# The prompt's down products of an expert in one run of sixteen matmuls, with two buffers of raw down weights

## What is computed

```python
def ec_moe(h, w_router, w_g, w_u, w_d):
    B, n, D = h.shape
    cap = EC_FACTOR * n // N_EXPERTS          # 256 sample tokens, 32 prompt tokens
    aff = jax.nn.softmax((h @ w_router).astype(jnp.float32), axis=-1)
    vals, idx = lax.top_k(aff.transpose(0, 2, 1), cap)
    xg = jax.vmap(lambda hb, ib: hb[ib])(h, idx)
    a = jnp.einsum('becd,edf->becf', xg, w_g)
    u = jnp.einsum('becd,edf->becf', xg, w_u)
    y = jnp.einsum('becf,efd->becd', jax.nn.silu(a) * u, w_d) * vals[..., None].astype(h.dtype)
    ...
```

## Time and profile before

| | us |
|---|---|
| median of 3 runs | 3077.3 (3075.81 to 3077.61) |
| span of the profiled execution | 3073.1 |
| PE busy in it | 2897.7 (94%) |
| PE's weight loads busy | 2284.8 (74%) |
| DVE busy | 1953.7 (64%) |
| ACT busy | 1085.5 (35%) |
| POOL busy | 1070.6 (35%) |

### The profile page before, as it was taken

The page is one execution under the profiler, slowest core; times in us unless marked ns, Lnnn a source line. Parts: engine busy times, 40 slices in busy tenths (PEclk is TensorE's granted clock), DMA queues, the critical chain, the costliest instruction groups (busy, mean ns, idle before and its releaser), DMA issues. The chain is left out here.

```text
span 3073.1 us, 42659 instructions
## 1 busy us (share of the span) xinstructions
PE 2897.7 (94%) x16288; PEld 2284.8 (74%) x16288; DVE 1953.7 (64%) x2559; ACT 1085.5 (35%) x1723; POOL 1070.6 (35%) x693
## 2 busy tenths in 40 slices
PE   6999999999889999999999999989977999999993
PEld 3888888888676666666666667878856888888882
DVE  5418292829438888888888866555575555555555
ACT  5311111111344444444444443223432333434344
POOL 1000000000105343443433554522136766666652
PEclk9999999999898999999999999999988999999996
DMA  6213222211441110110110117675534666666657
GB/s 235 102 50 108 79 102 79 100 73 61 171 152 32 27 33 7 32 33 7 34 26 6 55 53 226 182 248 179 168 135 140 199 205 200 194 204 211 205 186 291
DMA packets 139518, 371.25 MB, mean 121 GB/s; under 512 B 20886, under 2 KB 47996, under 8 KB 129116
## 3 DMA queue, kind: packets, MB, share of 16 engines
q1 hardware_dynamic: 99756, 266.55, 26.0%
q0 software_dynamic: 24048, 74.72, 8.6%
q10 hardware_dynamic: 15552, 27.79, 2.6%
HBM read 266.07 MB, written 102.89 MB: 120 GB/s over the span
## 5 line engine op out<-in xcount | busy, mean ns | idle before, releaser
L1209 ACT ACTIVATE at_w<-banks 128x512 f32<-128x512 f32 (+1 forms) x592 | 347.6, 591 | 463.6 <-PE banks L1316 407.9
L1432 DVE TENSOR_REDUCE at_mpart<-banks 128x1 f32<-128x512 f32 (+1 forms) x584 | 373.7, 682 | 136.5 <-PE banks L1343 136.5
L1288 POOL TENSOR_TENSOR at_part<-at_part,at_w 128x512 f32<-128x512 f32 x224 | 297.6, 1329 | 327.2 <-ACT at_w L1209 323.9
L2705 POOL TENSOR_TENSOR late<-moe_raw_gu,late 128x2048 fp32r<-128x2048 f32 x62 | 287.2, 4633 | 121.6 <-ACT late L2770 121.3
L536 DVE SCALAR_TENSOR_TENSOR fr_r<-fr_r,fr_dw 128x2334 f32<-128x2334 f32 x120 | 318.0, 2650 | 3.9
L393 PE MATMUL fr_po<-hT_hi,fr_w_hi 128*128 128x512 f32 (+1 forms) x800 | 297.3, 372 | 3.0 <-PE fr_po L393 1.8
L393 PE MATMUL fr_po<-hT_hi,fr_w_lo 128*128 128x512 f32 (+1 forms) x800 | 294.9, 369 | 0.0
L393 PE MATMUL fr_po<-hT_lo,fr_w_hi 128*128 128x512 f32 (+1 forms) x800 | 294.9, 369 | 0.0
L1354 PE MATMUL banks<-at_w,V 128*64 128x256 f32 (+1 forms) x2368 | 283.0, 381 | 0.0
L2897 DVE TENSOR_TENSOR late<-raw,late 128x1024 fp32r<-128x1024 f32 x64 | 192.0, 3001 | 100.8 <-ACT late L2809 100.8
L1458 DVE TENSOR_TENSOR at_part<-at_part,at_w 128x512 f32<-128x512 f32 x224 | 231.5, 1033 | 13.0
(11 more groups left out here) (404 smaller groups left out, 6295.6 us busy)
## 6 DMA issues: line engine op xcount, KB each, us to landing
moe_raw_gu<-w_gate_up SPq DMA_DIRECT2D x62, 1024.0 KB, 4.8
raw<-w_down SPq DMA_DIRECT2D x64, 512.0 KB, 4.0
fr_wm<-w_ada_rows POOLq DMA_DIRECT2D x32, 512.0 KB, 4.3
gates_scratch<-fr_r ACTq DMA_DIRECT2D x64, 256.0 KB, 2.0
mx_gates<-gates_scratch SPq DMA_DIRECT2D x64, 256.0 KB, 3.1
fr_raw<-w_in SPq DMA_DIRECT2D x28, 512.0 KB, 5.5
fr_r<-x POOLq DMA_DIRECT2D x18, 512.0 KB, 5.5
raw<-mixed_scratch SPq DMA_DIRECT2D x9, 1024.0 KB, 6.0
```

What stands on the lines that cost most here:

```text
L1209: act.activation(w[:, g % NW, k, 0:n], sc[:, (2 * g + k) % SCB, 0:n], ACT.Exp, scale=SM_SCALE).then_inc(exp_done, 1)
L1288: pool.tensor_tensor(part[:, j % 2, 1, 0:n], before, w[:, g % NW, 1, 0:n], ALU.add).then_inc(add_p, 1)
L1432: dve.tensor_reduce(mpart[:, s, tiles, c // 2], bank, AX.X, ALU.max).then_inc(red_done, 1)
L2705: pool.tensor_tensor(gu_lo[:, slot], raw_gu[:, slot], gu_hi[:, slot].bitcast(F32), ALU.subtract).then_inc(glo_done, 1)
```

## The change

The prompt's down products leave steps 1, 2 and 3. In step 0 of the next expert, behind the last piece's `down`, `down_prompt` now makes those of all four pieces in one run of 16 matmuls, still accumulating in `moe_y`, and raises the new semaphore `prompt_mm`. `d_mm` is raised by the last matmul of `down`. Since weights and activations must last until then, there is a second buffer of raw down weights (`raw_d[u]`) and `hid` holds four pieces of two experts. Room for it comes from the final phase: four of its nine tiles lie in `raw_d[0]`, and ACT's squares go to parts of `xg` and `hid`. SP's transfer of down weights waits for `prompt_mm` of two experts earlier in place of `d_mm`; `scale_y` waits for `prompt_mm`; the first `hid` of an expert waits for `prompt_mm` too.

```diff
-        gu_hi, gu_lo, raw_d = expert_buffers(raw, late)
+        gu_hi, gu_lo, raw_d0 = expert_buffers(raw, late)
+        raw_d = [raw_d0, p.sb("raw_d1", [P, M, D])]
...
-        act_g, hid = p.sb("act_g", [P, TOK]), p.sb("hid", [P, 2, TOK])
+        act_g, hid = p.sb("act_g", [P, TOK]), p.sb("hid", [P, 2, M, TOK])
...
-        fx, fsq = p.sb("fx", [P, U, D]), p.sb("fsq", [P, 2, D])
+        fx = p.sb("fx", [P, U - M, D])
+        fsq = [xg[:, 2], hid[:, 0].rearrange("p m n -> p (m n)")[:, 0:D]]
...
-                        sp.wait_ge(d_mm, q - 3)
-                        sp.dma_start(raw_d[:, m], t["w_down"][bass.ds(q * P, P), :]).then_inc(d_ld[m], 16)
+                        if not isinstance(e, int) or e > 1:
+                            sp.wait_ge(prompt_mm, e - 1)
+                        sp.dma_start(raw_d[u][:, m], t["w_down"][bass.ds(q * P, P), :]).then_inc(d_ld[m], 16)
...
                 def scale_y(e, u):
-                    dve.wait_ge(d_mm, M * e + M)
+                    dve.wait_ge(prompt_mm, e + 1)
...
+                        if m == 0 and (not isinstance(e, int) or e > 1):
+                            dve.wait_ge(prompt_mm, e - 1)
+                        dve.tensor_tensor(hid[:, u, m], bank[1][:, 0:TOK], act_g[:], ALU.mult).then_inc(hid_done, 1)
...
-                def down_prompt(slot, piece):
-
-                    for g in range(4):
-                        mm = pe.matmul(y3[g * CAPP:(g + 1) * CAPP, :], hid[:, slot, CAP:TOK], raw_d[:, piece, g * QD:(g + 1) * QD],
-                                       start=(piece == 0), stop=(piece == M - 1), skip_group_check=True)
                     mm.then_inc(d_mm, 1)
+
+                def down_prompt(u):
+
+                    for piece in range(M):
+                        for g in range(4):
+                            mm = pe.matmul(y3[g * CAPP:(g + 1) * CAPP, :], hid[:, u, piece, CAP:TOK],
+                                           raw_d[u][:, piece, g * QD:(g + 1) * QD],
+                                           start=(piece == 0), stop=(piece == M - 1), skip_group_check=True)
+                    mm.then_inc(prompt_mm, 1)
...
-                        if not (first and m == 0):
-                            down_prompt(1 - slot, (m - 1) % M)
+                        if m == 0 and not first:
+                            down_prompt(1 - u)
```

More of the change, by code:

```diff
@@ L2590, in moe_phase @@
         tp_done, xhi_done, xlo_done = p.sem("tp_done"), p.sem("xhi_done"), p.sem("xlo_done")
-        g_mm, u_mm, d_mm = p.sem("g_mm"), p.sem("u_mm"), p.sem("d_mm")
+        g_mm, u_mm, d_mm, prompt_mm = p.sem("g_mm"), p.sem("u_mm"), p.sem("d_mm"), p.sem("prompt_mm")
         silu_done, hid_done, hhi_done, hlo_done, y_done = (
@@ L2620, in buffer @@
             at = place_of(n)
-            return fx[:, at] if at < U else raw_gu[:, (at - U) // 2, (at - U) % 2].rearrange("p k n -> p (k n)")
+            if at < M:
+                return raw_d0[:, at]
+            return fx[:, at - M] if at < U else raw_gu[:, (at - U) // 2, (at - U) % 2].rearrange("p k n -> p (k n)")
         def wait_tab(eng, e):
@@ L2781, in squares @@
                     wait(act, sq_done, n - 1)
-                    act.activation(fsq[:, n % 2], buffer(n), ACT.Square, accum_out=sumsq[:, n:n + 1]).then_inc(sq_done, 1)
+                    act.activation(fsq[n % 2], buffer(n), ACT.Square, accum_out=sumsq[:, n:n + 1]).then_inc(sq_done, 1)
                 def rooted(n):
@@ L2808, in expert @@
                             act.wait_ge(d_mm, q - 1)
-                        act.activation(d_hi[:, slot], raw_d[:, m], ACT.Copy).then_inc(dhi_done, 1)
+                        act.activation(d_hi[:, slot], raw_d[u][:, m], ACT.Copy).then_inc(dhi_done, 1)
                         if last and m == M - 1:
@@ L2815, in expert @@
                         act.wait_ge(hid_done, q + 1)
-                        act.activation(h_hi[:, slot], hid[:, slot, 0:CAP], ACT.Copy).then_inc(hhi_done, 1)
+                        act.activation(h_hi[:, slot], hid[:, u, m, 0:CAP], ACT.Copy).then_inc(hhi_done, 1)
                         if m > 0 and not last:
@@ L2896, in expert @@
                         dve.wait_ge(dhi_done, q + 1)
-                        dve.tensor_tensor(d_lo[:, slot], raw_d[:, m], d_hi[:, slot].bitcast(F32), ALU.subtract
+                        dve.tensor_tensor(d_lo[:, slot], raw_d[u][:, m], d_hi[:, slot].bitcast(F32), ALU.subtract
                                           ).then_inc(dlo_done, 1)
@@ L2907, in expert @@
                             dve.wait_ge(d_mm, q - 1)
-                        dve.tensor_tensor(hid[:, slot], bank[1][:, 0:TOK], act_g[:], ALU.mult).then_inc(hid_done, 1)
+                        if m == 0 and (not isinstance(e, int) or e > 1):
+                            dve.wait_ge(prompt_mm, e - 1)
+                        dve.tensor_tensor(hid[:, u, m], bank[1][:, 0:TOK], act_g[:], ALU.mult).then_inc(hid_done, 1)
                         dve.wait_ge(hhi_done, q + 1)
-                        dve.tensor_tensor(h_lo[:, slot], hid[:, slot, 0:CAP], h_hi[:, slot].bitcast(F32), ALU.subtract
+                        dve.tensor_tensor(h_lo[:, slot], hid[:, u, m, 0:CAP], h_hi[:, slot].bitcast(F32), ALU.subtract
                                           ).then_inc(hlo_done, 1)
@@ L2954, in down @@
                             for n in range(2):
[L2955 to L2958, removed]
-                def down_prompt(slot, piece):
-                    for g in range(4):
-                        mm = pe.matmul(y3[g * CAPP:(g + 1) * CAPP, :], hid[:, slot, CAP:TOK], raw_d[:, piece, g * QD:(g + 1) * QD],
-                                       start=(piece == 0), stop=(piece == M - 1), skip_group_check=True)
-                    mm.then_inc(d_mm, 1)
+                                mm = pe.matmul(py[:, i, n * BLK:(n + 1) * BLK], h[:, slot, i * P:(i + 1) * P],
+                                               w[:, slot, n * BLK:(n + 1) * BLK],
+                                               start=(first_piece and h is h_hi and w is d_hi),
+                                               stop=(last_piece and h is h_lo))
+                    mm.then_inc(d_mm, 1)
+                def down_prompt(u):
[5 more added lines that the diff above has]
+                    mm.then_inc(prompt_mm, 1)
                 def keep_busy(count):
@@ L3017, in _ @@
                 down(1, False, True)
-                down_prompt(1, M - 1)
+                down_prompt(1)
                 pe.wait_ge(norm_ld, 16 * 6)
```

## The result

| | before | after |
|---|---|---|
| median of the runs, us | 3076.76 (3072.16 to 3079.55, 20 runs) | 3080.91 (3075.98 to 3095.56, 20 runs) |
| ratio to before | 1 | 1.0016, 95% interval 1.0009 to 1.0022 |
| span of the profiled execution, us | 3073.1 | 3084.0 |
| experts 2 to 14, us each | 42.62 | 42.93 |
| steps 0, 1, 2, 3 of one expert, us | 9.95, 10.81, 10.81, 11.05 | 11.25, 10.08, 10.53, 11.06 |

The change costs 0.16% (0.09 to 0.22%), 4 to 5 us. The time per expert is the distance of the gate products that start experts 2 and 15, over 13; the steps are distances of gate products within one expert.

A forecast was written before the change was run, and what follows sets the result against it. PE was taken to bound the loop, busy 42.50 of 42.62 us per expert. 13 x (1.30 - 1.00) = +3.9 and -0.02 for expert 15 gave a median of 3081.2 us, 8-in-10 range 3073.8 to 3085.8.

The forecast's parts named there:

- Pieces added: Step 0's prompt run: 0.43 us per further piece, 1.30 taken for three.
- Rival 3: Long run at step 0's end without overlap between pieces: 1.71 in place of 1.30, giving 3086.9 us; chance 0.10.
- Runs removed: Steps 1 to 3: a removed prompt run is worth 0.75 us where PE waits for nothing else.
- The wait at steps 2 to 3: PE's gate products wait some 0.4 us for DVE's token rests, so both first boundaries bring 1.00, not 1.50.
- Rival 1: No wait at steps 2 to 3, DVE's chain moves up with PE: 1.50 gained per expert, 3074.7 us; chance 0.13.
- Rival 4: Wait at steps 2 to 3 grows or shows at 1 to 2: 0.1 to 0.3 us more per expert; chance 0.14.
- Step 3 to 0: Boundary of step 3 and next step 0: removing the run gains nothing, as gate products wait for DVE.
- Rival 2: Every removed run pays in full, also at step 3 to 0: -12.4 us, giving 3064.9; chance 0.03.
- The ends: Expert 1's wait for POOL swallows earlier changes; expert 15 until ACT's rounding -0.02 us; DVE covers the last pieces.
- slack of 1.72: Step 0's end: `scale_y` waits 1.30 us longer, which fits into 1.72 before POOL's scatter, so no later scatter.
- -0.57 for the earlier release: Expert 15: ACT's last down-weight rounding, released by `down` instead of the prompt's run, starts 0.57 us earlier.
- some 3.9 us later than 3007.62: Sign to look for: start of ACT's rounding in expert 15, shifted by 3.9 us in the trace.

The follow-up runs named there:

- x1: Changed kernel with DVE's subtraction of down weights moved behind the first half of the token rests in steps 1 to 3: 3073.47 us, ratio 0.9987.
- x4: Kernel before without the prompt's runs of steps 1 to 3, step 0's run of 8 kept, pieces 0 to 2 left out: 3064.59 us, ratio 0.9959.
- x9: Changed kernel with POOL's subtraction of gate and up weights cut into two half-width instructions: 3076.64 us, ratio 0.9998.
- x5: Changed kernel with three prompt pieces at step 3's end, one in step 0, and DVE's down-weight subtraction behind the first token rests: 3064.99 us, ratio 0.9961.
- x6: Changed kernel with prompt pieces 0 to 2 at the end of step 3 and only piece 3 in the next step 0: 3073.57 us, ratio 0.9988.
- x7: Changed kernel with two prompt pieces at step 3's end, two in step 0, and DVE's down-weight subtraction behind the first token rests: 3065.58 us, ratio 0.9959.
- x3: Changed kernel's buffers, waits and earlier `d_mm`, but prompt's products still one piece at the end of every step: 3077.62 us, ratio 1.0004.
- x2: Kernel before with DVE's subtraction of down weights moved behind the first half of the token rests, as a control: 3077.58 us, ratio 1.0003.

## Why the prediction was right

**The loop, point by point.** The sum was +3.9 for experts 2 to 14; it is 13 x 0.303 = +3.94.

- Pieces added: 1.30 predicted for three; step 0 went from 9.95 to 11.25, and the run of 32 from 1.87 predicted to 1.86. Rival 3 (2.28 for that run) is out.
- Runs removed: 0.75 each where PE waits for nothing. Step 1 fell by 0.73. Step 2 falls by 0.76 where the wait is taken away (x1). Both boundaries together: 1.00 predicted, 0.73 + 0.28 = 1.01 in the kernel after, 1.00 in x4.
- The wait at steps 2 to 3: forecast at 0.4, against 0.50 between the two boundaries in the timeline of after; the transposes take 0.35 and not the 0.44 assumed, and the two gate matmuls behind them 0.35 (2537.72 to 2538.07) and not 0.27, so that the worth of a removed run came out right because two errors of some 0.09 cancel, and the wait came out 0.09 too short. That part was luck; the time of the step was not, since it hangs on when DVE ends, and that was 10.83 us after the transposes that end step 1 begin (2537.37 to 2548.20), with 10.85 forecast. PE started 0.06 after the rests, as forecast. Its cause is shown by x1 and x9, by two edits that have nothing in common but that DVE's rests come earlier. Rival 1 is out: its time per expert (42.42) is what x1 and x9 measure, but only with another order on DVE or another instruction on POOL. Rival 4 is out as well: it wanted 0.1 to 0.3 us more per expert than forecast, and the loop came out within 0.01.
- Step 3 to 0: unchanged, 11.05 and 11.06, with and without a run in it (x4). Rival 2 is out. That the slot is worth filling is the other side of the same reading; x5, x6 and x7 take it.

**The ends.** Expert 1 swallowed what was won before, the wait for POOL having grown from 3.31 to 3.87. Expert 15 and the final phase: -0.02 predicted until ACT's rounding, 29.93 against 30.00 us from the expert's start is -0.07; to the end 95.34 in all three profiles, against 95.38 and 96.31. One step of it was wrong in its reason. The slack of 1.72 between DVE and POOL's scatter was not all slack: POOL issued at 3003.64, 15.02 us after the expert's start in place of 14.64, so 0.38 later. It came to nothing because that first scatter took 2.10 us in place of the 2.50 of the earlier trace rows. And the -0.57 for the earlier release is right at ACT (x3: -0.61) and not shown beyond it, since the loads behind it may be later.

**What the prediction's signs got wrong.** It named ACT's rounding in expert 15 "some 3.9 us later than 3007.62". It was 10.93 later, at 3018.55:

```profile
3018.55 1.06 ACT L2814 ACTIVATE late<-moe_raw_d 128x1024 fp32r<-128x1024 f32 x1 [1.89 <-PE moe_py L2962]
```

The number compares two single executions across everything that stands before them, and the profile of before was an early one: again profiled, its span was 4.0 us longer. For the same reason its span of 3077.0 was missed (3084.0), and the median does not lie 4.2 above the span: the profiled execution of after took 3085.88 us, 1.9 more than its span, and the other 2.3 were the scatter between executions. The forecast of the median, made as a difference, does not suffer from that: 3081.2 against 3080.91 (+3.9 forecast, +4.2 by the medians, +4.9 by the ratio). That the two values lie only 0.3 apart is part luck: the median of three runs that it started from, 3077.3, is 0.5 above that of twenty.

## What to carry to other kernels

A small piece of work between two larger ones is to be priced by what comes behind it: it costs its full time and what a run of its own adds to it (0.75 us here together) where the next instruction is ready, and nothing where that one waits for another engine anyway. Collecting such pieces saves something at the first kind of place and throws away the cover at the second. So gather them, but put them down where the engine waits in any case, and look what the waits that they had covered hang on: x7 does both, for 0.4%.

When a sum is to be tested, compare distances between marks that repeat (a step, an expert), never times from the start of two executions: here the first agreed within 0.1 us over 13 experts, the second missed by 7 us, none of which the repeats tie to the change.

## What the runs showed of the hardware

- The same DVE subtraction (128x1024, two inputs in SBUF) took 4.79 us beside one POOL subtraction of 4.61, 2.58 beside one split in two, and 1.22 alone. It ended 1.07 to 1.08 us after the POOL instruction, or after its first half. Behind POOL instructions that follow without a gap, it was held for all that were left: 10.52 us across two whole ones (x1, expert 1), 7.35 us from the second of four halves on (x9, expert 1). `moe_hid`, with one input in PSUM, ran in 0.46 us beside POOL (x1).
- In the loop, splitting the POOL instruction made the pair take 5.74 us in place of 4.61; the second half took 3.38 us and the first 2.40, and the 1.13 us more of the pair are close to DVE's own 1.22.
- Behind an idle time of 3.3 to 3.9 us on PE, the granted clock fell to 1.2 GHz for 3.4 us in four executions and for 6.8 in one. The beginning differed too, by some 2 us, for the same wait. Each 3.4 us at half clock cost 1.3 to 1.5 us of the step (11.07, 12.4 to 12.6, 13.7). The profiles of x1 to x7 and x9 have the same fall in expert 1, for 3.4 us in x1, x2, x3, x4 and x6 and for 6.8 in x5, x7 and x9.
- A run of four column groups of 32 costs 0.43 us per further piece of eight records, from 8 to 32 records, and 0.32 (0.75 - 0.43) more for being a run of its own.
